# One kernel, two changes: the decay attention's level products cut to the blocks that their masks keep, and the FFNs' sums of the modulation moved to stage boundaries

## What is computed

```python
cond = jax.nn.silu(c)
mod = jnp.einsum('bd,sde->sbe', cond, ada_w[layer]) + ada_b[layer][:, None, :]   # e: 3 * 1024
shift, scale, gate = jnp.split(mod[0], 3, axis=-1)
h = rms_norm(x, norm_g[layer, 0]) * (1.0 + scale[:, None, :]) + shift[:, None, :]
```

```python
cum = jnp.cumsum(lf_c, axis=2)
rel = jnp.where(causal[:, :, None], cum[:, :, :, None, :] - cum[:, :, None, :, :], -jnp.inf)
attn = jnp.einsum('bhtd,bhsd,bhtsd->bhts', q_c, k_c, jnp.exp(rel))
o = attn @ v_c + jnp.einsum('bhtd,bhde->bhte', q_c * jnp.exp(cum), S)
```

## Time and profile before

| | |
|---|---|
| median of 3 runs | 3320.66 us (3316.99 to 3329.31) |
| the profiled execution | 3326.29 us |
| its span, first to last instruction | 3324.4 us |
| mean granted TensorE clock | 0.981 |
| busy: PE, DVE, ACT, POOL | 96%, 62%, 43%, 10% of the span |
| level phase of hgrn | 2721 to 2935 us |

### The profile page before, as it was taken

The page is one execution under the profiler, slowest core; times in us unless marked ns, Lnnn a source line. Parts: engine busy times, 40 slices in busy tenths (PEclk is TensorE's granted clock), DMA queues, the critical chain, the costliest instruction groups (busy, mean ns, idle before and its releaser), DMA issues. The chain is left out here.

```text
span 3324.4 us, 40625 instructions
## 1 busy us (share of the span) xinstructions
PE 3204.6 (96%) x15644; PEld 2575.3 (77%) x15644; DVE 2050.0 (62%) x2698; ACT 1435.8 (43%) x1938; POOL 319.5 (10%) x233
## 2 busy tenths in 40 slices
PE   7999999999999999999999989899999989999998
PEld 6888786788878888767788878556788778877887
DVE  5454427455445554436555554664899868868997
ACT  4222225322223222325322232473688647646885
POOL 0000000000000000000000000251143400002434
PEclk9999999999989999999999989899999999999999
DMA  5332221333223332232433223300999931219998
GB/s 197 146 151 95 100 90 52 133 152 133 114 82 146 152 134 93 106 141 33 171 149 140 109 80 129 83 1 26 375 414 412 307 101 61 64 44 382 413 414 301
DMA packets 99992, 534.18 MB, mean 161 GB/s; under 512 B 22000, under 2 KB 22896, under 8 KB 51456
## 3 DMA queue, kind: packets, MB, share of 16 engines
q1 hardware_dynamic: 89472, 494.37, 39.3%
q0 software_dynamic: 6624, 24.12, 2.6%
q10 hardware_dynamic: 3744, 13.63, 1.0%
HBM read 511.02 MB, written 31.02 MB: 163 GB/s over the span
## 5 line engine op out<-in xcount | busy, mean ns | idle before, releaser
L454 ACT ACTIVATE ffn_silu_gate<-ffn_gate_up 128x512 f32<-128x512 f32 x88 | 52.6, 598 | 937.4 <-PE ffn_gate_up L117 937.4
L516 DVE TENSOR_TENSOR ffn_product<-ffn_silu_gate,ffn_gate_up 128x512 f32<-128x512 f32 x88 | 60.5, 688 | 542.4 <-ACT ffn_silu_gate L454 542.4
L2890 DVE TENSOR_TENSOR moe_low<-moe_raw,moe_high 128x2048 fp32r<-128x2048 f32 x144 | 344.6, 2412 | 19.4 <-ACT moe_high L2758 18.8
L115 PE MATMUL ffn_down<-ffn_down_high,ffn_hid_high 128*128 128x512 f32 x704 | 278.8, 396 | 3.1 <-DVE x_tok L540 3.1
L2758 ACT ACTIVATE moe_high<-moe_raw 128x2048 fp32r<-128x2048 f32 x144 | 274.2, 1917 | 12.4 <-PE moe_bank L117 10.3
L540 DVE SCALAR_TENSOR_TENSOR x_tok<-ffn_down,x_tok 128x512 f32<-128x512 f32 x352 | 231.6, 685 | 75.3 <-PE ffn_down L117 71.9
L116 PE MATMUL ffn_down<-ffn_down_low,ffn_hid_high 128*128 128x512 f32 x704 | 277.5, 394 | 0.0
L117 PE MATMUL ffn_down<-ffn_down_high,ffn_hid_low 128*128 128x512 f32 x704 | 277.1, 394 | 0.0
L115 PE MATMUL ffn_gate_up<-ffn_h_high,w 128*128 128x512 f32 x704 | 276.6, 393 | 0.0
L116 PE MATMUL ffn_gate_up<-ffn_h_low,w 128*128 128x512 f32 x704 | 274.4, 390 | 0.0
L117 PE MATMUL ffn_gate_up<-ffn_h_high,w 128*128 128x512 f32 x704 | 274.2, 389 | 0.0
(11 more groups left out here) (640 smaller groups left out, 7365.1 us busy)
## 6 DMA issues: line engine op xcount, KB each, us to landing
moe_raw<-in_moe_w SPq DMA_DIRECT2D x192, 1024.0 KB, 8.6
ffn_raw_gate_up<-in_ffn_gate_up SPq DMA_DIRECT2D x85, 1024.0 KB, 6.0
ffn_ada_w<-in_ada_w SPq DMA_DIRECT2D x32, 1536.0 KB, 7.0
...
```

The costliest lines, as they stand in the source:

```text
L115: pe.matmul(out, lhsT[0], rhs[0], start=first, stop=False)
L454: act.activation(silu_gate[slot][:, :], gate_up_ps[2 * slot][:, :], ACT.Silu).then_inc(silu_done, 1)
L516: dve.tensor_tensor(product[slot][:, :], silu_gate[slot][:, :], gate_up_ps[2 * slot + 1][:, :], ALU.mult)\
L2890: dve.tensor_tensor(low[n % SPLITS][:, :, :], raw[n % RAWS][:, :, :], high[n % SPLITS][:, :, :].bitcast(FP32), ALU.subtract)\
```

## The change

Modulation. The 24 matmuls and the two VectorE operations become two helpers, `sum_modulation` and `take_modulation`. The sum now takes 64 columns of `ada_acc` at a time, into the lower or upper half of the partitions, so 48 float32 matmuls. They leave the end of the FFN and go to the first instructions of the next stage on PE (mixer_0, mixer_1, and ffn1_1 for the part that ffn2_0 collected); only the last FFN does its own, behind its last `down`, with the VectorE part at the stage's very end. `ada_acc` gets a fixed place in SBUF that lives across the boundary; the mixer's `o_tok` and first `scores` buffer lie over it. New waits: PE waits for `before_ready` ahead of the projections (the sum's bank is used again), SP waits for it ahead of `store_modulation`, the first write of `ada_acc` in ffn1_1 waits for the sum.

Levels. For the diagonal and sizes 1 to 16 (`NEAR_LEVELS`), everything kept lies in 32x32 blocks on the diagonal: PE makes 16 matmuls a unit (4 chunks x 4 blocks, 32 columns of weights, 32 moving), and VectorE's masked copy is 128x128 in all instead of 128x512, into a small `near_att`. Size 32 is 2 blocks of 32x32 a chunk (8 matmuls) and size 64 one of 64x64 (4 matmuls), copied without a mask. GpSimd copies a head's near blocks into `att` (4 copies a head), and `output` waits for that.

```diff
@@ -54,2 +54,4 @@
         self.stored = ctx.enter_context(nc.semaphore("stored"))
+        with nc.sbuf_tensor("ada_acc", [P, 3 * DM], FP32) as buffer:
+            self.ada_acc = buffer
 
@@ -291,2 +293,22 @@
 
+def sum_modulation(pe, chip, ada_acc, bank, summed):
+
+    for j in range(3 * KT):
+        for part in range(2):
+            rows, at = slice(64 * part, 64 * part + 64), j * P + 64 * part
+            last = pe.matmul(bank[rows, j:j + 1], ada_acc[:, at:at + 64], chip.ones[:, 0:1], start=True, stop=True)
+    last.then_inc(summed, 1)
+
+
+def take_modulation(dve, chip, part, bank, summed, ready):
+
+    mod = chip.mod[:, part, :, :]
+    bias = chip.gain("ada_b_2", part).rearrange("p (a k) -> p a k", a=3)
+    dve.wait_ge(summed, 1)
+    dve.tensor_tensor(mod, bank[:, 0:3 * KT].rearrange("p (a k) -> p a k", a=3), bias, ALU.add).then_inc(ready, 1)
+    dve.wait_ge(ready, 1)
+    dve.scalar_tensor_tensor(out=chip.mod_gain[:, part, :], in0=mod[:, 1, :], scalar=1.0,
+                             in1=chip.gain("norm_g_2", part), op0=ALU.add, op1=ALU.mult).then_inc(ready, 1)
+
+
 NFT = DFF // P
@@ -295,3 +317,3 @@
 
-def ffn(chip, name, which, gain, next_chunk, final=False):
+def ffn(chip, name, which, gain, next_chunk, before=None, final=False):
 
...
@@ -332,5 +356,5 @@
         ada_w = [s.sb(f"ada_w{i}", [P, 3 * DM]) for i in range(2)]
-        ada_acc = s.sb("ada_acc", [P, 3 * DM])
         ada_loaded = [s.sem(f"ada_loaded{i}") for i in range(2)]
         ada_added, ada_summed, mod_ready = s.sem("ada_added"), s.sem("ada_summed"), s.sem("mod_ready")
+        before_summed, before_ready = s.sem("before_summed"), s.sem("before_ready")
 
@@ -382,3 +406,7 @@
         def _(pe):
+            if before is not None:
+                sum_modulation(pe, chip, ada_acc, gate_up_ps[3], before_summed)
             norm.turn_first(pe)
+            if before is not None:
+                pe.wait_ge(before_ready, 1)
 
@@ -429,9 +457,6 @@
                 down(2 * i + 1, (2, 3))
-            pe.wait_ge(ada_added, KT)
-            pe.wait_ge(product_ready, NFT)
-            for j in range(3 * KT):
-                last = pe.matmul(gate_up_ps[0][:, j:j + 1], ada_acc[:, j * P:(j + 1) * P], chip.ones[:, 0:1],
-                                 start=True, stop=True)
-            last.then_inc(ada_summed, 1)
             down(NCHUNK - 1, (0, 1))
+            if final:
+                pe.wait_ge(ada_added, KT)
+                sum_modulation(pe, chip, ada_acc, gate_up_ps[0], ada_summed)
 
@@ -508,2 +533,4 @@
             norm.vector(dve)
+            if before is not None:
+                take_modulation(dve, chip, before, gate_up_ps[3], before_summed, before_ready)
             norm.vector_evacuate(dve, gain)
@@ -550,2 +577,4 @@
                 else:
+                    if before is not None:
+                        dve.wait_ge(before_summed, 1)
                     dve.tensor_scalar(ada_acc[:, :], ada_w[slot][:, :], chip.cond[:, 0:1], None, ALU.mult)\
@@ -573,11 +602,2 @@
             step(NFT - 1, 1, False, add=(NCHUNK - 2,))
-            dve.wait_ge(ada_summed, 1)
-            mod = chip.mod[:, which, :, :]
-            bias = chip.gain("ada_b_2", which).rearrange("p (a k) -> p a k", a=3)
-            dve.tensor_tensor(mod, gate_up_ps[0][:, 0:3 * KT].rearrange("p (a k) -> p a k", a=3), bias, ALU.add)\
-                .then_inc(mod_ready, 1)
-            dve.wait_ge(mod_ready, 1)
-            dve.scalar_tensor_tensor(out=chip.mod_gain[:, which, :], in0=mod[:, 1, :], scalar=1.0,
-                                     in1=chip.gain("norm_g_2", which), op0=ALU.add, op1=ALU.mult)\
-                .then_inc(mod_ready, 1)
             split_gate_up(NFT, 0)
@@ -612,5 +632,8 @@
                 final_scale(3)
+                take_modulation(dve, chip, which, gate_up_ps[0], ada_summed, mod_ready)
+                dve.wait_ge(mod_ready, 2)
             else:
                 add_some(0, 8, NCHUNK - 1)
-            dve.wait_ge(mod_ready, 2)
+                if before is not None:
+                    dve.wait_ge(before_ready, 2)
 
@@ -836,3 +859,3 @@
 
-def mixer(chip, name, layer, lam_init, next_chunk):
+def mixer(chip, name, layer, lam_init, next_chunk, before):
 
...
@@ -879,3 +904,3 @@
         mixT = [s.sb(f"mixedT{i}", [P, TT, P]) for i in range(2)]
-        o_tok = s.sb("o_tok", [P, TT, HEADS, P])
+        before_summed, before_ready = s.sem("before_summed"), s.sem("before_ready")
         lam = s.sb("lam", [P, 8])
@@ -947,2 +972,3 @@
             weights.fill(sp, 4)
+            sp.wait_ge(before_ready, 2)
             if layer == 0:
@@ -958,3 +984,5 @@
         def _(pe):
+            sum_modulation(pe, chip, ada_acc, banks.ps[3], before_summed)
             norm.turn_first(pe)
+            pe.wait_ge(before_ready, 1)
             weights.project(pe, 0, 0, norm.high, norm.low, True, norm)
@@ -1122,2 +1150,3 @@
             norm.vector(dve)
+            take_modulation(dve, chip, before, banks.ps[3], before_summed, before_ready)
             norm.vector_evacuate(dve, chip.gain("mix_norm", layer))
@@ -1768,2 +1797,4 @@
 LEVELS = [None] + [1 << l for l in range(7)]
+BLOCK = 32
+NEAR_LEVELS = [b for b in LEVELS if b is None or 2 * b <= BLOCK]
 
@@ -1810,2 +1841,3 @@
         att = s.sb("att", [P, 2, TT, P])
+        near_att = s.sb("near_att", [P, 2, TT, BLOCK])
         M = [s.sb(f"decayed{i}", [P, SEQ]) for i in range(3)]
@@ -1815,3 +1847,3 @@
         squares = s.sb("squares", [P, P])
-        masks = s.sb("masks", [P, len(LEVELS) - 1, P], I32)
+        masks = s.sb("masks", [P, len(NEAR_LEVELS), BLOCK], I32)
         keep = s.sb("keep", [P, SEQ])
@@ -1829,2 +1861,3 @@
         level_done, level_taken, att_zeroed = s.sem("level_done"), s.sem("level_taken"), s.sem("att_zeroed")
+        near_placed = s.sem("near_placed")
         cum_exp, last_gaps, last_exp, q_decayed, k_decayed = [
...
@@ -1890,3 +1926,12 @@
             pool.wait_ge(norm.turned, KT)
+            pool.memset(near_att[:, :, :, :], 0.0).then_inc(att_zeroed, 1)
             pool.memset(att[:, :, :, :], 0.0).then_inc(att_zeroed, 1)
+            pool.wait_ge(att_zeroed, 2)
+            for h in range(HG):
+                pool.wait_ge(level_taken, 8 * h + len(NEAR_LEVELS))
+                if h >= 2:
+                    pool.wait_ge(o_done, h - 1)
+                for j in range(P // BLOCK):
+                    at = block_of(j)
+                    pool.tensor_copy(att[at, h % 2, :, at], near_att[at, h % 2, :, :]).then_inc(near_placed, 1)
 
@@ -1933,4 +1978,11 @@
                     pe.wait_ge(level_taken, u - 1)
+                bank = level_ps[u % 2]
                 for c in range(TT):
-                    last = pe.matmul(level_ps[u % 2][:, tokens(c)], left[:, tokens(c)], right[:, tokens(c)], start=True, stop=True)
+                    if size in NEAR_LEVELS:
+                        tiles = [(BLOCK * j, BLOCK * j, BLOCK) for j in range(P // BLOCK)]
+                    else:
+                        tiles = [(j, j + size, size) for j in range(0, P, 2 * size)]
+                    for keys_at, queries_at, n in tiles:
+                        last = pe.matmul(bank[keys_at:keys_at + n, c * n:c * n + n], left[:, c * P + keys_at:c * P + keys_at + n],
+                                         right[:, c * P + queries_at:c * P + queries_at + n], start=True, stop=True)
                 last.then_inc(level_done, 1)
@@ -1955,2 +2007,3 @@
                 pe.wait_ge(level_taken, 8 * h + 8)
+                pe.wait_ge(near_placed, 4 * h + 4)
                 if h > 0:
@@ -2210,9 +2263,18 @@
                 dve.wait_ge(level_done, u + 1)
-                mask = chip.ident[:, :].bitcast(I32) if size is None else masks[:, LEVELS.index(size) - 1, :]
+                bank = level_ps[u % 2]
+                if u > 0:
+                    dve.wait_ge(level_taken, u)
                 if u == 8 * h and h >= 2:
+                    dve.wait_ge(near_placed, 4 * (h - 1))
+                if u == 8 * h + len(NEAR_LEVELS) and h >= 2:
                     dve.wait_ge(o_done, h - 1)
-                elif u > 0:
-                    dve.wait_ge(level_taken, u)
-                dve.copy_predicated(att[:, h % 2, :, :], mask.unsqueeze(1).broadcast_to([P, TT, P]),
-                                    level_ps[u % 2][:, :].rearrange("p (c t) -> p c t", c=TT)).then_inc(level_taken, 1)
+                if size in NEAR_LEVELS:
+                    mask = masks[:, NEAR_LEVELS.index(size), :].unsqueeze(1).broadcast_to([P, TT, BLOCK])
+                    ins = dve.copy_predicated(near_att[:, h % 2, :, :], mask,
+                                              bank[:, 0:TT * BLOCK].rearrange("p (c t) -> p c t", c=TT))
+                else:
+                    for j in range(0, P, 2 * size):
+                        ins = dve.tensor_copy(att[j:j + size, h % 2, :, j + size:j + 2 * size],
+                                              bank[j:j + size, 0:TT * size].rearrange("p (c t) -> p c t", c=TT))
```

(10 more changed lines are left out.)

20 lines of the change are left out of this document (13 added, 7 removed).

## The result

The changed kernel takes 3279.64 us (median of 4, 3278.97 to 3287.86) against 3321.51 us; the ratio is 0.9865, interval [0.9847, 0.9884], so 45 us less by the ratio, between 38 and 51, and 41.9 by the medians. Forecast were 3272 and a range of 3260 to 3297. Measured again beside the experiments, it took 3285.1 us against 3323.8, ratio 0.9889 [0.9875, 0.9904], 38.7 less by the medians: the two intervals overlap in a small part, and a gain of 37 to 45 us is what can be said. The sum had 48.5.

The account below looks back on a forecast made before the run. PE was taken to bound the kernel, busy in 96% of the span, with DVE second in the level phase. -30.9 - 17.6 = -48.5 us, from the median of 3320.7 to 3272; range 3260 to 3297.

Parts of the forecast that it names:

- part A: Modulation sums moved from the FFNs' ends to stage starts and the last FFN's end: -30.9 us.
- part B: Decay attention's level products cut to the kept blocks, near units at 0.0126 us a pass: -17.6 us.
- (1): Level passes have a floor near 0.025 to 0.029 us with all 128 rows: 3293 us; chance 0.16.
- (2): Sums at starts run at half rate and `down` waits for DVE in each FFN: 3282 us; chance 0.12.
- FFN ends, -34.3: Without sums ahead of the last `down`, four FFN ends fall from 77.91 us to 10.90 each: -34.3 us.
- Starts, +3.0: Sums at mixer_0, ffn1_1 and mixer_1 starts, 96 passes at 0.029: 1.0 us each, 3 in all.
- End of ffn2_1, +0.4: Last FFN: sums hide behind the last `down`, DVE's two operations at the stage's end add 0.4 us.
- the switch that falls away: Level phase: in 16 of 64 ticks no projection stands between levels, saving 0.25 us more about 14 times: -3.5.
- all sizes at 0.0126: Level phase: every size's passes at 0.0126 us makes part B -24 us.
- (3): Level phase: PE's instructions come too slowly, 20 blocks each holding PE 4.12 us: +82, 3353 us; chance 0.04.
- PE's 6.5 idle us can only shrink; I count nothing: Level phase: with less DVE work PE's idle time can't grow; counted as nothing, bound -4 us.
- What would make it wrong: DVE bounding the level phase, additions holding up the last `down`, or small passes lowering the clock: 12 x 0.2 us per projection part.

Follow-up runs that it names:

- part A alone: Only the sums of the modulation moved, against the kernel before, with its level products unchanged; 3298.24 us, ratio 0.9927.
- e4: Changed kernel with ACT's order in a tick changed: keys' exponential and turned keys' copy right behind the tick's decays; 3276.32 us, ratio 0.9855.
- e5: Changed kernel, in near units the four chunks of one 32-column position in a row instead of positions in turn; 3286.5 us, single run.
- e6: Changed kernel with size 64 as two products of 32 columns by 64 instead of one of 64 by 64; 3283.25 us, ratio 0.9869.
- e9: Changed kernel with the edits of both e4 and e6; 3276.37 us, ratio 0.9851.
- run 24: Not a run's number: the text says that part A alone, in its own run, took 24 us less than the kernel before; 3298.24 us.
- e12: e4's kernel with every FFN's sums behind its last `down` instead of at the next stage's start; 3279.77 us, ratio 0.9862.
- e3: Only the level products cut to the kept blocks, against the kernel before, with its sums unmoved; 3312.83 us, ratio 0.9967.
- e7: Changed kernel with the sums at the starts in four groups of 32 columns instead of two of 64; 3286.97 us, ratio 0.9879.
- e11: Changed kernel with the sums at their new places in 48 passes of 128 columns instead of 96 of 64; 3299.34 us, ratio 0.992.

## Why the prediction was right, and where it was off

The measured time lies in the range of 3260 to 3297, and part A came near its terms; of part B's gain about half was lost. That the range held in spite of this is partly luck: 3279.6 us is at the edge of the 3264 to 3280 for both parts near their terms and 3285.1 outside it, and the room above was left for rivals (1) and (2), neither of which happened.

**FFN ends, -34.3.** 77.91 us became 4 x (10.67 + 0.23) = 43.6: -34.3. The additions held nothing up; DVE's split (2.28) and the additions behind it ran beside the products as the prediction had laid out.

**Starts, +3.0.** +1.1 in both profiles of the changed kernel (64.17 and 64.16 against 63.05), +4.2 in part A alone, +1.3 to +2.7 in the profiles of e4, e5, e6 and e9. The 0.029 a pass of the earlier trace rows held: 2.77 us for 96. The bounds (0.3 and 9) and the reason for the spread, the clock's fall during the sums, were right.

**End of ffn2_1, +0.4.** +0.9: from the last scaling's end to the start of nsa it was 1.3 us, now 2.2. The two operations' waits weigh more than the operations, within the bound of 1.

**Part A.** By these terms -32.3 against -30.9; in its own run 24 less (20 to 29). Where the remaining few microseconds of that run went is open, but for the 2.9 more in `down`.

**Part B, the passes.** 0.0126 was taken for a pass of four positions, 0.0085 was measured; rival (1)'s floor doesn't hold in this order, and would nearly have held in e5's. A near tick with a projection gained 0.29 to 0.36 instead of 0.24. The near tick without one gained 0.31 (1.56 to 1.25), where the sum had 0.24 and 0.25 for the switch that falls away, and the pair of sizes 32 and 64 gained 0.60, where it had 0.32, nothing and the same 0.25. Size 64 was put at 0.080 a pass "as loads can't overlap there"; it took 0.065, and its weight loads, 0.138 us each, start every 0.058, so they do overlap. In all 19.8 instead of 17.6 us of PE's work. Two figures beside the sum were slightly off: all sizes at 0.0126 make -22.8, not -24, and (3) 3354, not 3353.

**Part B, the step that failed:** "PE's 6.5 idle us can only shrink; I count nothing". They grew from 5.5 to 11.5, and the clock fell behind them. Of 17.6 forecast, 7.9 to 10.6 came, and this is nearly the whole difference between 48.5 and the 41.9 and 38.7 measured by the medians. The prediction had weighed PE's shorter ticks against DVE's total (182.8 of 214) and looked at ACT not at all, as its 136 us are less still. A total is the wrong figure: ACT was full for stretches of 14 to 18 us with no gap over 0.06 us in them (in the trace of before), and the earlier trace rows can't show that. The waits for ACT and DVE were in the trace of before already (L1949 2.3 us, L1943 1.7): each of them grew by what PE's work ahead of it, since ACT's stretch began, had lost: 1.56 to 2.75, 0.70 to 1.93 and 1.70 to 3.15, so 1.2 to 1.5 us, about four or five ticks of 0.3.

**DVE and GpSimd.** DVE's busy time fell by 21.0 (25 forecast), masked copies 0.296 (0.3), 64x256 0.417 (0.42). GpSimd's copies were 0.546 each inside bounds of 0.2 and 1; no PE wait names them, only L2012 behind DVE's states, 0.4.

**What would make it wrong** named DVE as a bound and the clock in the level phase. The clock did fall there, but behind waits, not because the passes are small: with e4's order and the same passes it stays full in e4 and e9, and in e12 it falls once, for 3.4 us, again behind a wait.

## The fastest version

e4 (3276.32) and e9 (3276.37) are the fastest; e4 is the changed kernel with its own ACT order, 8.8 us below it by the medians of runs made together. Beside the first measurement of the changed kernel (0.9865 [0.9847, 0.9884]) the intervals overlap, so the gain rests on the phases in the profiles, 191.65 and 191.60 us, and 193.16 in e12, which has the same order, against 198.3 to 202.5 in the six profiles with the levels cut and the old order (the changed kernel's two, e3, e6, e7 and e11).
